# Two transformer blocks on one core: a weight ring of six places whose low halves lie over the landed weights

## What is computed

```python
for l in range(DEPTH):
    h = rmsnorm(x, g_mix_pre[l])
    (a_q, a_k, a_v, b_cq, b_ckv, b_kr, c_q, c_k, c_v) = jnp.split(h @ w_in[l], IN_SPLITS, axis=-1)
    ...
    mix = jnp.concatenate([o_a, o_b, o_c], axis=-1) @ w_out[l]
    x = x + rmsnorm(mix, g_mix_post[l])
    xo = cross_attention(rmsnorm(x, g_x_pre[l]), rmsnorm(mem, g_x_mem[l]), w_xq[l], w_xkv[l], w_xo[l])
    x = x + rmsnorm(xo, g_x_post[l])
    gate, up = jnp.split(rmsnorm(x, g_ffn_pre[l]) @ w_ffn_in[l], 2, axis=-1)
    f = (jax.nn.silu(gate) * up) @ w_ffn_out[l]
    x = x + rmsnorm(f, g_ffn_post[l])
```

```python
x = half_step_ffn(x, m[:, 0], m[:, 1], m[:, 2], ffn_w_in[i, 0], ffn_w_out[i, 0], ln_g[i, 0], ln_b[i, 0])
...
x = post_norm_update(x, y_lat, m[:, 5], 1.0, ln_g[i, 1], ln_b[i, 1])
...
x = half_step_ffn(x, m[:, 6], m[:, 7], m[:, 8], ffn_w_in[i, 1], ffn_w_out[i, 1], ln_g[i, 2], ln_b[i, 2])
```

## Time and profile before

| | us |
|---|---|
| three runs | 2393.53, 2401.67, 2404.04 (median 2401.67) |
| the profiled execution | 2394.3 |
| its span | 2392.5 |
| PE, DVE, ACT, POOL at work | 2190.3, 914.3, 1092.5, 1699.5 |

### The profile page before, as it was taken

One profiled execution on the slowest core, in us unless ns is written; L12 is line 12 of the kernel. 1 busy time (PEld: TensorE's weight loads), 2 busy tenths in 40 slices (PEclk: granted clock), 3 DMA queues, 4 the chain that ended last, 5 costly groups with the idle time before them and its releaser, 6 DMA issues.

```text
span 2392.5 us, 32266 instructions
## 1 busy us (share of the span) xinstructions
PE 2190.3 (92%) x10151; PEld 1757.1 (73%) x10151; DVE 914.3 (38%) x1802; ACT 1092.5 (46%) x1671; POOL 1699.5 (71%) x1367
## 2 busy tenths in 40 slices
PE   5998999999988998898999899998988998878986
PEld 4886777678876776776777677786876877666875
DVE  5355656544545333443433324443104110443102
ACT  4554454345644543443444344555534443435432
POOL 5746388776454986786788779627876987767975
PEclk9999999999999999999999999999999999989998
DMA  6425377654354878676687765424654665444653
GB/s 202 141 106 187 130 246 264 228 173 149 107 176 133 283 246 267 214 264 241 237 275 268 259 187 155 141 89 149 186 178 130 200 185 179 138 152 144 190 176 104
DMA packets 135701, 447.08 MB, mean 187 GB/s; under 512 B 22506, under 2 KB 28098, under 8 KB 135608
## 3 DMA queue, kind: packets, MB, share of 16 engines
q1 hardware_dynamic: 128920, 426.62, 54.3%
q10 hardware_dynamic: 6688, 19.23, 2.4%
HBM read 444.60 MB, written 3.03 MB: 187 GB/s over the span
## 4 chain that ended last, share of the span: by engine, by line
POOL 50%; issue 31%; PE 14%; DVE 2%; POOLq 1%; ACT 1%; DMA 1%; SPq 0%; DVEq 0%; ACTq 0%
POOL w_lo L756 49%; PE ps L1952 3%; PE ps L1954 3%; PE ps L1953 3%; PE ps L2396 1%; PE ps L2361 1%; PE ps L2384 1%; PE ps L2215 1%; POOLq L177 0%; DMA land<-w_in_dram 0%; PE ps L2357 0%; POOLq L754 0%; POOL ada_land L802 0%; PE ps L2226 0%; PE ps L2327 0%
## 5 line engine op out<-in xcount | busy, mean ns | idle before, releaser
L756 POOL TENSOR_TENSOR w_lo<-land,w_hi 128x512 fp32r<-128x512 f32 x1308 | 1663.4, 1303 | 634.5 <-ACT w_hi L848 633.2
L848 ACT ACTIVATE w_hi<-land 128x1024 fp32r<-128x1024 f32 x654 | 689.8, 1059 | 929.8 <-PE ps L1954 736.0
L1952 PE MATMUL ps<-w_hi,h_hi 128*128 128x512 f32 (+1 forms) x1872 | 753.4, 402 | 70.6 <-DVE h_lo L1412 39.4
L1954 PE MATMUL ps<-w_hi,h_lo 128*128 128x512 f32 (+1 forms) x1872 | 737.8, 394 | 0.0
L1953 PE MATMUL ps<-w_lo,h_hi 128*128 128x512 f32 (+1 forms) x1872 | 736.9, 394 | 0.0
L1952 PEld LDWEIGHTS ps<-w_hi,h_hi 128*128 128x128 f32 x1872 | 356.9, 191 | 178.8 <-issue 58.1
L1954 PEld LDWEIGHTS ps<-w_hi,h_lo 128*128 128x128 f32 x1872 | 356.6, 190 | 76.9
L1953 PEld LDWEIGHTS ps<-w_lo,h_hi 128*128 128x128 f32 x1872 | 357.3, 191 | 69.6
L1952 PE MATMUL ps<-w_hi,hid_hi 128*128 128x512 f32 x616 | 253.0, 411 | 52.9 <-POOL w_lo L756 43.2
L1435 DVE TENSOR_TENSOR hid_lo<-ps,hid_hi 128x512 f32 (+1 forms) x77 | 53.2, 691 | 634.0 <-ACT hid_hi L989 634.0
L1953 PE MATMUL ps<-w_lo,hid_hi 128*128 128x512 f32 x616 | 248.5, 403 | 0.0
(11 more groups left out here) (259 smaller groups left out, 1870.6 us busy)
## 6 DMA issues: line engine op xcount, KB each, us to landing
land<-ffn_w_in_dram SPq DMA_DIRECT2D x220, 512.0 KB, 3.6
ada_land<-ada_w_dram SPq DMA_DIRECT2D x144, 512.0 KB, 5.2
land<-ffn_w_out_dram SPq DMA_DIRECT2D x110, 512.0 KB, 3.9
land<-w_ffn_in_dram SPq DMA_DIRECT2D x88, 512.0 KB, 3.8
land<-w_ffn_out_dram SPq DMA_DIRECT2D x44, 512.0 KB, 5.0
land<-na_w_qkv_dram SPq DMA_DIRECT2D x40, 512.0 KB, 4.2
land<-w_xkv_dram SPq DMA_DIRECT2D x32, 512.0 KB, 3.5
land<-w_in_dram SPq DMA_DIRECT2D x32, 488.0 KB, 3.4
```

Source lines behind the costliest of these rows:

```text
L756: done = pool.tensor_tensor(w_lo[:, slot, half], land[:, slot, half], w_hi[:, slot, half].bitcast(F32), ALU.subtract)
L848: act.activation(w_hi[:, slot, :], land[:, slot, :], ACT.Copy).then_inc(*my.up("hi_ready"))
L1952: pe.matmul(dst, lh, wh, start=first, stop=False)
L1954: done = pe.matmul(dst, ll, wh, start=False, stop=last)
```

## The change

- `RING` is 6. `land` is allocated, its memory is given back, and `w_lo` is allocated over it; POOL subtracts in place. SP's transfer of unit u waits for PE's use of unit u-6.
- ACT's `split(RING)` at the start issues six; other calls that named `RING` keep four (`split(4)`, `split(8)`, `los(seen[0] + 4)`).
- `w_in` units are split at their 976 columns instead of 1024 (`WIDTHS`).
- `ffn_out`: three half-width units (`HALF_FIRST`) before the last `turn_hid` instead of four; the wait for all `split_lo` before them is gone. The store of adaLN's sums comes six units after the first, not four.
- The loops of `ffn_in` and of `products` are written out.
- `load_tables` still follows the first four units; `biases` follow the first six.
- `tables_v` becomes `angles` (before the first `zin`) and `distances`; `tables` and `distances` stand behind `m_lo`, with fewer and longer instructions.

```diff
-RING = 4
+RING = 6
+HALF_FIRST = 3
...
-        land = sb("land", [P, RING, UW])
+        with ExitStack() as below:
+            land = sb("land", [P, RING, UW], F32, below)
+        w_lo = sb("w_lo", [P, RING, UW], F32R)
         w_hi = sb("w_hi", [P, RING, UW], F32R)
-        w_lo = sb("w_lo", [P, RING, UW], F32R)
...
                     if u - RING + 1 > 0:
-                        sp.wait_ge(sems["lo_ready"], my.at("lo_ready", u - RING + 1))
+                        sp.wait_ge(sems["w_used"], my.at("w_used", u - RING + 1))
                     sp.dma_start(land[:, slot, 0:width], at).then_inc(*my.up(f"landed{slot}", 16))
...
-                    while done < RING:
+                    while done < asked[0][0]:
                         unit(src[first + done])
                         done += 1
                     while asked:
-                        asked.pop(0)()
+                        asked.pop(0)[1]()
...
             def na_tables():
-                asked.append(load_tables)
+                asked.append((4, load_tables))
...
-                    asked.append(biases)
+                    asked.append((RING, biases))
...
-                    act.activation(w_hi[:, slot, :], land[:, slot, :], ACT.Copy).then_inc(*my.up("hi_ready"))
+                    act.activation(w_hi[:, slot, 0:WIDTHS[u]], land[:, slot, 0:WIDTHS[u]], ACT.Copy).then_inc(*my.up("hi_ready"))
...
             def products_in(l):
                 dve.wait_ge(*my.last())
+                if l == 0:
+                    angles()
                 scaled_out("zin", 0, IN_GW, 0, R_X, "taken")
-                if l == 0:
-                    tables()
                 scaled_out("zin", 1, IN_GW, 1, R_X, "taken")
...
+                if l == 0:
+                    tables()
+                    distances()
                 dve.wait_ge(sems["w_used"], my.at("w_used", n["w_used"] + 4))
                 rope_keys()
...
-                first = 4
-                pe.wait_ge(sems["split_lo"], my.at("split_lo", n["split_lo"]))
+                first = HALF_FIRST
                 pe.wait_ge(sems["taken"], my.at("taken", n["taken"] - 1))
```

More of the change, by code:

```diff
@@ L292, in build @@
             "start_in",
-            "landed0", "landed1", "landed2", "landed3",
+            *(f"landed{j}" for j in range(RING)),
             "hi_ready",
@@ L505, in build, with run @@
         UNITS = sum(counted)
+        NARROW = []
+        forward({"products": lambda w, groups, width, dst, **kw: NARROW.extend([UW] * 4 * groups), "products_y": lambda w, **kw: NARROW.extend([UW] * 8),
+                 "products_in": lambda l: NARROW.extend([2 * IN_GW] * 16), "kv_weights": lambda w: NARROW.extend([UW] * KV_UNITS),
+                 "products_q": lambda w: NARROW.extend([UW] * 8), "products_na": lambda: NARROW.extend([UW] * 4 * NA_GROUPS),
+                 "ffn_in": lambda w, **kw: NARROW.extend([UW] * 4 * FG), "ffn_out": lambda w, **kw: NARROW.extend([UW] * FC)})
+        WIDTHS = tuple(NARROW)
+        assert len(WIDTHS) == UNITS
+        def run(u, count):
+            n = 0
+            while n < count and WIDTHS[u + n] == WIDTHS[u]:
+                n += 1
+            return n
         def ada_vectors(g):
@@ L619, in stream @@
                 if times:
-                    with my.turns(times, units=RING, lo_ready=RING, **{f"landed{s}": 16 for s in range(RING)}) as i:
+                    with my.turns(times, units=RING, w_used=RING, **{f"landed{s}": 16 for s in range(RING)}) as i:
                         for j in range(RING):
@@ L626, in stream, with ada_extra @@
                     done += 1
-            def ada_extra(starts):
+            def ada_extra(starts, lag=4):
                 extra = {}
@@ L664, in ffn_in @@
                 assert ada_vectors(g0 + times - 1) == ada_vectors(g0 - 1) == both and stored[0] == g0 - 1
-                with my.turns(times, units=8, lo_ready=8, ada_steps=KC * both, ada_sum=1, ada_stored=16, ada_bias_in=16 * both,
-                              **{f"ada_in{j}": 16 for j in range(4)}, **{f"landed{s}": 32 for s in range(RING)}) as i:
+                for i in range(times):
                     for k in range(8):
@@ L754, in lo @@
                 pool.wait_ge(sems["hi_ready"], my.next("hi_ready"))
-                for half in (slice(0, UW // 2), slice(UW // 2, UW)):
+                width = WIDTHS[u]
+                for half in (slice(0, width // 2), slice(width // 2, width)):
                     done = pool.tensor_tensor(w_lo[:, slot, half], land[:, slot, half], w_hi[:, slot, half].bitcast(F32), ALU.subtract)
@@ L761, in los @@
             def los(until):
[L763 to L770, removed]
+                while my.n["units"] < min(until, UNITS):
+                    count = run(my.n["units"], min(until, UNITS) - my.n["units"])
+                    if count >= 2 * RING:
+                        with my.turns(count // RING, units=RING, hi_ready=RING, lo_ready=RING):
+                            for _ in range(RING):
+                                lo()
+                        count %= RING
+                    for _ in range(count):
+                        lo()
             def units(count):
@@ L847, in unit @@
                         act.wait_ge(sems["w_used"], my.at("w_used", u - RING + 1))
-                    act.activation(w_hi[:, slot, :], land[:, slot, :], ACT.Copy).then_inc(*my.up("hi_ready"))
+                    act.activation(w_hi[:, slot, 0:WIDTHS[u]], land[:, slot, 0:WIDTHS[u]], ACT.Copy).then_inc(*my.up("hi_ready"))
                 count = min(count, UNITS - n["units"])
-                while count and (my.turn is not None or n["units"] < RING or count < 2 * RING):
+                while count and (n["units"] < RING or run(n["units"], count) < 2 * RING):
                     unit()
                     count -= 1
-                if count >= 2 * RING:
-                    with my.turns(count // RING, units=RING, w_used=RING, hi_ready=RING,
+                if count:
+                    alike = run(n["units"], count)
+                    count -= alike // RING * RING
+                    with my.turns(alike // RING, units=RING, w_used=RING, hi_ready=RING,
                                   **{f"landed{s}": 16 for s in range(RING)}):
@@ L858, in split @@
                             unit()
-                    count %= RING
                 for _ in range(count):
@@ L912, in products_in @@
             def products_in(l):
[L913 removed]
+                split(8)
                 if l == 0:
@@ L991, in ffn_in @@
                 split(4)
[L992 to L997, removed]
+                for g in range(FG - 1):
+                    silu(g)
+                    split(4)
+                    split_hid(g, slice(2 * g, 2 * g + 2))
                 silu(FG - 1)
@@ L2098, in products @@
                     return
[L2099 to L2103, removed]
+                for g in range(2, groups):
+                    pe.wait_ge(sems["taken"], my.at("taken", n["taken"] - 1))
+                    group((g % 2, g % 2 + 2), width)
+                    n["taken"] += 1
             def products_y(w, keys=False, ada_load=False, sums=False, done=0):
@@ L2141, in ffn_in @@
                 n["taken"] += 1
[L2142 to L2150, removed]
+                for g in range(1, FG):
+                    pe.wait_ge(sems["taken"], my.at("taken", n["taken"] - 1))
+                    group((g % 2, g % 2 + 2), GW)
+                    turn_hid(g - 1)
+                    n["taken"] += 1
+                    if ada and g % 2 == 0:
                         ada_sum()
-                        ada_at[0] += times - 1
             def ffn_out(w, ada=(), columns=None, then=None):
```

71 lines of the change are left out of this document (32 added, 39 removed).

## The result

| | before | changed |
|---|---|---|
| median of four runs, us | 2402.63 | 2495.27 |
| lowest and highest | 2393.53, 2404.04 | 2483.92, 2495.63 |
| span of the profiled execution | 2392.5 | 2493.8 |
| mean granted clock of PE | 0.97 | 0.946 |

The changed kernel takes 1.039 times as long (95% interval 1.035 to 1.043), 93 us more by the medians and 101.3 by the two profiled spans. The forecast was slower, 2445, and the range ended at 2480: the sign was right and the size about half of what came.

A forecast was written before the change was run, and what follows sets the result against it. PE was busy 2190.3 of 2392.5 us, with the chain of waits through POOL's subtraction (50%). Gains of about 59 and costs of 112 gave 53 us slower than 2394.3, stated as 2445; 8-in-10 range 2362 to 2480.

The forecast's parts named there:

- clock terms: PE at half clock behind its waits: less of it at ffn_out, more at stage ends (+8), mixers and na's tables.
- the tables: Before na_w_qkv, SP's small table transfers delay the fifth unit; PE starts 17.5 us late, 2 for the clock: 19 lost.
- The gain at ffn_out: At six ffn_out places, PE's waits for POOL and the half clock behind them go: 40 us gained, bounds 0 and 53.
- The new wait of PE for DVE's bank: In ffn_out, PE reaches a bank DVE must still empty: 1.6 us at three places, 2.6 at three, 12.6 lost.
- The landing: Wherever ACT's order was just in time, work behind a `w_hi` comes one landing later, 3.6 us less the slack.
- an rms end: Stage end where ACT's squares follow a late `w_hi`: 3.2 us lost at one, 2.8 each at four others.
- rival 3: PE idle for 5 us some 45 times, each followed by half clock: slower, 2487 us; chance 0.08.
- Other waits for POOL: PE's waits for POOL outside the counted ffn_out places shrink: 19 us gained, bounds 8 and 27.
- The mixer's stall: In mixer and attention, ACT's `w_hi` waits for unit 36, exponentials behind it; PE loses 7 there, 34 over both layers.
- The start: Six `w_hi` before the first `h_hi` and longer clearing cost 3 to 4, reordered tables offset: 0, bounds -6 and +6.

The follow-up runs named there:

- the rms ends alone: The changed kernel with one `w_hi` instead of three before the squares at rms ends, the other two after the last `h_hi`; 2467.1 us, 1.028 of before.
- four units ahead: The changed kernel with `split(4)` instead of `split(RING)` at the start, ring of six kept; 2366.4 us, 0.989 of before.
- the fastest kernel: The changed kernel with `split(4)` at the start, two `w_hi` added before the last `hid_hi` of ffn_in and two fewer in ffn_out; 2353.96 us, 0.985 of before.
- five units ahead: The changed kernel with `split(5)` at the start instead of six; 2395.24 us, 0.998 of before.
- three half-width units alone: The kernel before, ring of four, with three half-width units instead of four in ffn_out and no `split_lo` wait before them; 2368.06 us, 0.988 of before.

## Why the prediction was half right

**The mechanism** was the forecast's: a `w_hi` two units further on, whose transfer starts at the event that was waited for before. Shown by four, five and six units ahead and by the rms ends alone.

**The step that failed** is the size of two terms. The sum was 48 us short of the 101 between the traces. The forecast's clock terms come to -1 in all (+8 at the ends, +4 at the mixers, +2 at the tables, -12 at ffn_out, -3 behind the two other waits for POOL); PE's busy time grew by 25.8. That is 27 of the 48. The other 21 is idle time: longer landings at the ends of stages, and waits for POOL that gave back less.

**The gain at ffn_out** (forecast 40, measured 37) was right in sum by luck. I gave it to six finished units together with three half-width units; but three half-width units, without the wait for `split_lo`, gain 38 in the old ring, and the ring of six with four units ahead only 3 more. Depth pays with a lead that is local: 56. In the changed kernel what the lead could add is not there. The new wait of PE for DVE's bank, which I put at 1.6 and 2.6, is: 0.9 to 1.2 at the first four places and 1.9 to 2.3 at the last three.

```profile
1202.98 0.50 PE L1967 MATMUL ps<-w_hi,hid_hi 128*128 128x512 f32 x1 [0.89 <-DVE hid L1557]
```

With four units ahead and in the fastest kernel it is gone; that `silu` there no longer stands behind a `w_hi` that waits for its landing would explain it.

**The landing.** I priced each place at 3.6 us of issue to landing less slack, with 2.8 to 3.2 for an rms end. ACT and SP there, in the changed kernel, to be held against the earlier trace rows:

```profile
226.62 1.06 ACT L860 ACTIVATE w_hi<-land 128x1024 fp32r<-128x1024 f32 x1 [4.25 <-DMA land<-w_xq_dram]
229.30 1.06 ACT L860 ACTIVATE w_hi<-land 128x1024 fp32r<-128x1024 f32 x1 [1.62 <-DMA land<-w_xq_dram]
230.93 1.06 ACT L860 ACTIVATE w_hi<-land 128x1024 fp32r<-128x1024 f32 x1 [0.57 <-DMA land<-w_xq_dram]
231.89 0.58 ACT L1105 ACTIVATE rows<-ps 128x512 f32<-128x512 f32 x1
...
223.04 4.42 SPq L615 DMA_DIRECT2D land<-w_xq_dram  x4
...
233.92 0.77 PE L1967 MATMUL ps<-w_hi,h_hi 128*128 128x512 f32 x1 [5.95 <-DVE h_lo L1424]
```

The landings of the four transfers that SP issues there from 223.04 on:

```profile
DMA to landing us min/median/max: 3.6/4.9/5.1
```

The last half passes release a unit every 1.36 us. Four transfers of 512 KB then leave at that distance (385 GB/s if none were to queue), and only the first lands in 3.6, as ACT's `w_hi` at 226.62 shows; the others take 4.9 to 5.1. The squares stand behind the third. So PE waits 5.95 - 1.80 = 4.15 more here and not 3.1. At the five rms ends the waits are 5.7 to 6.8, 22.8 us more in sum where 14.4 were forecast; the other 10 of the 33 in the table are half clock. The quiet median of the earlier trace rows was the wrong row, and it should have been seen from the distance of the releases. The estimate of 3.2 us that the prediction works out from the Trainium skill (DMA: Bandwidth & Descriptors, Anatomy of one DMA) is further off than 3.6; the fit there is for transfers issued by GpSimd, and these are SP's.

**The clock.** PE's time at work at half clock went from 103 us to 166, although of 37 us of half clock at the six ffn_out places only 7 are left. Behind the wait of 5.95 PE stands at half clock for the next 5 us, where before, behind 1.80, it kept the full clock (the changed kernel first, then the kernel before, same view as the earlier trace rows):

```profile
233.90:238.90 5.00, 4.98 (x12) 3.94 (x13) 4.25 (x11) 0.58 (x1) 3.98 (x4) 0.50 0.00 0
```

```profile
205.20:210.20 5.00, 4.82 (x20) 3.68 (x21) 4.18 (x11) 0.62 (x1) 4.43 (x4) 1.00 0.67 211
```

Twelve products in 5 us against twenty. This was rival 3 (0.08 in the forecast): its mechanism ran, and with 2487 it came nearer to 2495 than the forecast did, though not by its own count. It took 45 waits of 5 us; PE has 23 of over 4 us, where it had 11. And 45 places at 2 instead of 0.8 us are 54, not the 40 in its sum. No length of wait is shown from which the half clock sets in: before the change PE was at half clock behind a wait of 2.19 us and kept the full clock behind one of 2.94. The Trainium skill (TensorE: Matmul & The Clock Gate, HAM oscillation) describes waits that cool the clock each time, and here it was the nearer guide for the long waits.

**Other waits for POOL**, 19 forecast and 8 come, though POOL is waited for 47 us less. Of the 8, 6 are given back in ffn_in stages and 3 in the short convolution, nearly all directly behind a dear end of a stage, so as part of the loss before. That gain and the costs were not to be added.

**Right as worked out**: the tables, 17.5 and 2 forecast, 18.9 measured. SP's and ACT's rows, to be held against the earlier trace rows:

```profile
1474.75 1.70 SPq L615 DMA_DIRECT2D land<-na_w_qkv_dram  x2
...
1477.74 15.20 SPq L709 DMA_DIRECT2D ada_land<-rpb_w  x24
1493.30 0.97 SPq L615 DMA_DIRECT2D land<-na_w_qkv_dram  x2
...
1496.91 1.06 ACT L860 ACTIVATE w_hi<-land 128x1024 fp32r<-128x1024 f32 x1 [15.23 <-DMA land<-na_w_qkv_dram]
...
1499.44 0.79 PE L1967 MATMUL ps<-w_hi,h_hi 128*128 128x512 f32 x1 [20.61 <-ACT z L1153]
```

The mixer's stall, too (41 us with its attention where 34 were forecast), is the one foreseen at the earlier trace rows: ACT's `w_hi` waits for unit 36, and PE 6.71 us for the exponentials behind it.

```profile
170.17 0.43 SPq L615 DMA_DIRECT2D land<-w_out_dram  x1
...
174.88 1.06 ACT L860 ACTIVATE w_hi<-land 128x1024 fp32r<-128x1024 f32 x1 [9.75 <-DMA land<-w_out_dram]
...
176.47 3.67 PE L2405 MATMUL ps<-zin,probT 128*128 128x64 f32 x16 [6.71 <-ACT probT L1242]
```

The start is 5 us late by the seventeenth unit, and 3.6 with four `w_hi` in front; what of that is the longer clearing and what the tables' work was not taken apart. How much of the mixers' 41 us is the stall at unit 36 was not tried alone; with five units ahead the mixers cost 5 us over the kernel before.

## What to carry to other kernels

A deeper ring and a longer lead in an engine's program are two changes. The lead belongs only where the engine will stand for something long (here before the last `hid_hi` of ffn_in); anywhere else it puts other work behind an event that is not due yet. When a wait moves from the middle of a pipeline to its end, price a transfer by the rate at which places are then freed, not by the landing of one alone, and ask of every wait that grows whether PE runs at half clock behind it.

## What was not expected of the hardware

The subtraction in place costs POOL nothing: 1292 ns a piece against 1303, 32 of the 654 units being narrower. And in the neighbourhood attention, where PE is busy and waits for nothing long, executions differ in clock: over 55 us of it one kernel was granted 0.81 and another, with the same program there, 1.00. The first is that with three half-width units alone, the second the kernel before:

```profile
1520.00:1575.00 55.00, 53.31 (x360) 45.20 (x360) 29.72 (x69) 29.29 (x71) 12.43 (x10) 0.81 0.26 77
```

```profile
1535.00:1590.00 55.00, 53.13 (x439) 45.70 (x437) 34.41 (x81) 34.96 (x81) 15.10 (x12) 1.00 0.26 78
```

From the last unit before the attention to the first behind it the one takes 69.0 us and the other 59.4, so such a stretch costs some 10 us. The traffic of the transfers is the same in both. It may be a part of why single runs of a kernel spread by 10 to 20 us; what starts it, these runs do not show.
